# Attention logits from float32r operands, with the decay rows in two parts, and head-pair copies moved one place up in the order

## The reference, cut to what matters

```
log_f = log_sigmoid(f_logit)                       # (tokens, heads)
cum   = cumsum(log_f over tokens)                  # per head
s     = q_t . k_s / sqrt(64) + (cum[t] - cum[s])   # logits, blocks of 128 query tokens
s     = where(s_pos <= t_pos, s, -inf)             # causal
p     = softmax(s);  out = p @ v
y_b   = out @ attn_w_out
merged = sigmoid(g_a) * y_a + sigmoid(g_b) * y_b ; merged @ w_out
```

## Time and profile before

| | us |
|---|---|
| median of 3 runs | 2123.0 (2119.06 to 2129.02) |
| the profiled execution's own time | 2125.95 |
| its span, first to last instruction | 2124.2 |
| TensorE busy in the span | 1950.9 (92%) |
| VectorE busy | 1540.6 (73%) |
| ScalarE busy | 984.4 (46%) |

### The profile page before, as it was taken

How to read it: one execution, slowest core, us unless ns; L and a number is a source line. 1 busy time by engine, 2 the same in 40 slices (tenths; PEclk the granted TensorE clock), 3 DMA queues, 4 the chain that set the end, 5 groups by cost and what they waited for, 6 DMA issues and landing times.

```text
span 2124.2 us, 34037 instructions
## 1 busy us (share of the span) xinstructions
PE 1950.9 (92%) x14000; PEld 1813.8 (85%) x14000; DVE 1540.6 (73%) x2265; ACT 984.4 (46%) x1551; POOL 245.0 (12%) x190
## 2 busy tenths in 40 slices
PE   6897999987979998998889998999899989998998
PEld 6796899987958997988879888998898889888997
DVE  5866688878556897688667666898777667666555
ACT  5523444454235444545443455444546543445444
POOL 1020011110201111111100000111111100001111
PEclk9998999989989999999989999999999989999999
DMA  5320599523215984445523345896444523244552
GB/s 206 119 98 21 195 341 359 215 100 114 85 54 225 357 328 166 169 161 236 234 103 120 120 156 208 339 374 252 145 172 170 183 96 140 100 169 147 181 179 100
DMA packets 53291, 384.23 MB, mean 181 GB/s; under 512 B 5904, under 2 KB 6032, under 8 KB 6928
## 3 DMA queue, kind: packets, MB, share of 16 engines
q1 hardware_dynamic: 53136, 382.05, 48.1%
HBM read 380.98 MB, written 1.05 MB: 180 GB/s over the span
## 4 chain that ended last, share of the span: by engine, by line
PE 72%; DVE 16%; ACT 6%; issue 4%; DMA 1%; SPq 0%; DVEq 0%; ACTq 0%
PE stream L436 14%; PE stream L437 14%; PE stream L438 14%; PE works L450 5%; PE works L451 5%; PE works L452 5%; DVE w_lo L1030 3%; ACT w_hi L775 3%; DVE mx L1139 2%; DMA raw<-w 1%; PE stream L488 1%; DVE mx L1227 1%; PE works L612 1%; PE stream L489 1%; PE works L697 1%
## 5 line engine op out<-in xcount | busy, mean ns | idle before, releaser
L436 PE MATMUL stream<-h_hi,w_hi 128*128 128x256 f32 x2976 | 854.5, 287 | 23.5 <-DVE w_lo L1030 23.3
L437 PE MATMUL stream<-h_lo,w_hi 128*128 128x256 f32 x2976 | 847.9, 285 | 0.0
L438 PE MATMUL stream<-h_hi,w_lo 128*128 128x256 f32 x2976 | 847.6, 285 | 0.0
L1030 DVE TENSOR_TENSOR w_lo<-raw,w_hi 128x1024 fp32r<-128x1024 f32 x572 | 736.2, 1308 | 145.8 <-ACT w_hi L775 119.4
L775 ACT ACTIVATE w_hi<-raw 128x1024 fp32r<-128x1024 f32 x572 | 588.3, 1050 | 131.7 <-PE works L452 82.0
L436 PEld LDWEIGHTS stream<-h_hi,w_hi 128*128 128x128 f32 x2976 | 576.9, 194 | 32.8 <-issue 29.9
L437 PEld LDWEIGHTS stream<-h_lo,w_hi 128*128 128x128 f32 x2976 | 577.3, 194 | 2.6 <-issue 0.5
L438 PEld LDWEIGHTS stream<-h_hi,w_lo 128*128 128x128 f32 x2976 | 576.9, 194 | 0.0
L1506 POOL TENSOR_TENSOR g_lo<-hid,g_hi 128x256 fp32r<-128x256 f32 x140 | 191.9, 1372 | 1589.9 <-ACT g_hi L805 1589.9
L933 ACT ACTIVATE gate_t<-stream 128x256 f32<-128x256 f32 x132 | 50.6, 384 | 408.0 <-PE stream L438 405.2
L450 PE MATMUL works<-w_hi,g_hi 128*128 128x512 f32 x528 | 207.5, 393 | 4.2 <-DVE w_lo L1030 4.1
(11 more groups left out here) (368 smaller groups left out, 2271.1 us busy)
## 6 DMA issues: line engine op xcount, KB each, us to landing
raw<-w SPq DMA_DIRECT2D x294, 1024.0 KB, 4.8
mx<-w SPq DMA_DIRECT2D x64, 1024.0 KB, 7.0
par<-p_in SPq DMA_DIRECT2D x2, 1110.0 KB, 7.5
x<-x_in SPq DMA_DIRECT2D x1, 1024.0 KB, 6.7
mx<-bt_in SPq DMA_DIRECT2D x2, 512.0 KB, 5.6
out<-x SPq DMA_DIRECT2D x4, 256.0 KB, 2.4
con<-const_in SPq DMA_DIRECT2D x1, 968.0 KB, 4.7
par<-p_in SPq DMA_DIRECT2D x1, 225.0 KB, 6.8
```

Source lines behind the costliest of these rows:

```text
L436: mm(o, hi, r_hi[:, kt, :], start=first, stop=False, skip_group_check=True)
L437: mm(o, hi, r_lo[:, kt, :], start=False, stop=False, skip_group_check=True)
L438: last = mm(o, lo, r_hi[:, kt, :], start=False, stop=end, skip_group_check=True)
L1030: v.tensor_tensor(w_lo[:, q % SLOTS, :], raw[:, chunk_of_unit[q] % RAWS, (q % 2) * UNIT:(q % 2 + 1) * UNIT], w_hi[:, q % SLOTS, :].bitcast ...
```

## The change

Three things change in the mixers of both second-kind layers, and one in the constant table.

1. The identity and one 128x128 penalty block are rounded to float32r tiles (`ident_r`, `pen_r`) by two ScalarE copies at the start of the program. The decay rows get a tile of their own, `cum_r`, with a high and a low part of 384 columns each, zeroed by one VectorE memset. At `cum`, ScalarE writes the high part as before; VectorE then waits for it and writes the low part (two instructions on 8 partitions).
2. `score` has five products instead of four: high part, low part (384 columns each) and penalty (256 columns, the one block read twice) as float32r products; the two products of q and k stay as they are. TensorE also waits for the low part and the two rounded tables.
3. `hout` 1 moves in front of `pair` 15, `hout` 2 in front of `glu` 1.
4. The constant table loses two blocks of the penalty and half of the row of times: 1552 columns instead of 1936, in the first transfer of the program.

```diff
-    ("pair", 15), ("norm_p", 6), ("score", 7), ("hout", 1), ("attend", 4), ("turnp", 5),
-    ("glu", 0), ("norm_p", 7), ("attend", 5), ("turnp", 6),
-    ("glu", 1), ("hout", 2), ("attend", 6), ("turnp", 7), ("hsplit", 0),
+    ("hout", 1), ("pair", 15), ("norm_p", 6), ("score", 7), ("attend", 4), ("turnp", 5),
+    ("glu", 0), ("norm_p", 7), ("attend", 5), ("turnp", 6), ("hout", 2),
+    ("glu", 1), ("attend", 6), ("turnp", 7), ("hsplit", 0),
...
-PC, NC = columns([("ident", P), ("triu", P), ("ones", P), ("m", 7 * P), ("pen", 3 * P), ("time", T), ("c", 8),
+PC, NC = columns([("ident", P), ("triu", P), ("ones", P), ("m", 7 * P), ("pen", P), ("time", T // 2), ("c", 8),
...
+        ident_r = sb("ident_r", [P, P], F32R)
+        pen_r = sb("pen_r", [P, P], F32R)
+        cum_r = sb("cum_r", [P, 2, 384], F32R)
...
-        cumrows = p2_(0, "c_im")[:, 0:384]
+        cum_hi, cum_lo = cum_r[:, 0, :], cum_r[:, 1, :]
...
                     pe.wait_ge(s_cm_done, 2 * (L + 1))
+                    pe.wait_ge(s_cl_done, 2 * (L + 1))
+                    pe.wait_ge(s_masks_done, 2)
...
-                    mm(o[:, 0:384], ident[:, i:i + 1].to_broadcast([P, P]), cumrows, start=True, stop=False,
-                       skip_group_check=True)
-                    mm(o[:, P:384], ident, c_("pen", P), start=False, stop=False, skip_group_check=True)
+                    pick = ident_r[:, i:i + 1].to_broadcast([P, P])
+                    mm(o[:, 0:384], pick, cum_hi, start=True, stop=False, skip_group_check=True)
+                    mm(o[:, 0:384], pick, cum_lo, start=False, stop=False, skip_group_check=True)
+                    mm(o[:, P:384].rearrange("p (a n) -> p a n", a=2), ident_r[:], pen_r[:].unsqueeze(1).to_broadcast([P, 2, P]),
+                       start=False, stop=False, skip_group_check=True)
...
+            f(ident_r[:], ident, ACT.Copy).then_inc(s_masks_done, 1)
+            f(pen_r[:], c_("pen"), ACT.Copy).then_inc(s_masks_done, 1)
...
-                        f(cumrows[0:8, a:a + n_], works[0:8, 2, 0:n_], ACT.Copy, scale=-1.0).then_inc(s_cm_done, 1)
+                        f(cum_hi[0:8, a:a + n_], works[0:8, 2, 0:n_], ACT.Copy, scale=-1.0)\
+                            .then_inc(s_cm_done, 1)
...
-                    v.memset(cumrows, 0.0).then_inc(s_cum_zero, 1)
+                    v.memset(cum_r[:].bitcast(F32), 0.0).then_inc(s_cum_zero, 1)
...
+                elif kind == "cum":
+                    dve.wait_ge(s_cm_done, 2 * (L + 1))
+                    dve.wait_ge(s_cum_zero, L + 1)
+                    for a, n_ in ((0, T), (T, P)):
+                        v.scalar_tensor_tensor(cum_lo[0:8, a:a + n_], works[0:8, 2, 0:n_], -1.0,
+                                               cum_hi[0:8, a:a + n_].bitcast(F32), ALU.mult, ALU.subtract).then_inc(s_cl_done, 1)
```

More of the change, by code:

```diff
@@ L328, in build @@
          s_pe_f, s_f_dve, s_f_act, s_lf_done, s_pe_ck, s_cm_done, s_pe_vt, s_vt_sb, s_pe_sc,
-         s_bu_half, s_cum_zero, s_y_out, s_nm_done, s_p_exp, s_p_norm, s_pe_pt, s_pt_sb, s_pe_at, s_pads, s_dt_done) = (
+         s_masks_done, s_cl_done, s_bu_half, s_cum_zero, s_y_out, s_nm_done, s_p_exp, s_p_norm, s_pe_pt, s_pt_sb, s_pe_at, s_pads, s_dt_done) = (
             sem(n) for n in """pe_stat sq_done hf_done hhi_done hlo_done gate_th hid_done ghi_done glo_done
@@ L337, in build @@
             tab_sin pe_bu z_sum z_in wv_done s_sum pe_y g_in g_tanh
-            pe_f f_dve f_act lf_done pe_ck cm_done pe_vt vt_sb pe_sc bu_half cum_zero y_out nm_done p_exp p_norm
+            pe_f f_dve f_act lf_done pe_ck cm_done pe_vt vt_sb pe_sc masks_done cl_done bu_half cum_zero y_out nm_done p_exp p_norm
             pe_pt pt_sb pe_at pads dt_done""".split())
@@ L1617 @@
         "ident": np.eye(P), "triu": (idx[:, None] <= idx[None, :]), "ones": np.ones((P, P)),
-        "m": np.concatenate(masks, axis=1), "pen": -np.concatenate([np.zeros((P, P)), future, future], axis=1),
-        "time": np.broadcast_to(np.arange(T)[None, :], (P, T)), "c": tiles(a["c_2"][0]),
+        "m": np.concatenate(masks, axis=1), "pen": -future,
+        "time": np.broadcast_to(np.arange(BLK)[None, :], (P, BLK)), "c": tiles(a["c_2"][0]),
         "final": tiles(a["final_norm_g"])})
```

## The result

The changed kernel took 2112.95 us as a median of 7 runs (2109.08 to 2114.48). The kernel before, run beside it, took 2129.02 us (2119.06 to 2133.53, 7 runs). The ratio is 0.9921, with a 95% interval of 0.9904 to 0.9939: 16.8 us faster. The prediction was 2104.0 us with a range up to 2112: the measured time lies 1 us outside it. The saving had been forecast as 19.3 us.

The account below looks back on a forecast made before the run. TensorE was taken to bound the mixers; savings of 9.8 + 7.5 + 1.5 + 0.5 = 19.3 us from 2125.95 gave 2106.7, and 2.95 less as a median gave 2103.7, predicted as 2104 us, range 2097 to 2112.

Parts of the forecast that it names:

- The products of the logits: In each of 16 scores, three float32r products take 0.56 us instead of 1.17, saving 9.8 us in all.
- third: In the scores, exposed weight loads make the new products cost 1.12 us; 0.8 us saved, 2113 us; chance 0.04.
- fourth rival: In the scores, float32r on spread or repeated operands costs as much as float32, losing 10.2 us; 2125 us; chance 0.04.
- the second: Scores gain less than TensorE saves because VectorE is still busy; half of 9.8 us lost, 2109 us; chance 0.07.
- The copies moved up: At attend 4 and 6 in both mixers, the waits for the hout copy go, saving 7.5 us.
- the first rival: The wait moves on to attend 5 and 6 in both mixers, costing 4 us; 2108 us; chance 0.15.
- The clock: Behind the first mixer's wait at attend 4, the fall to half clock goes too: 1.5 us, bounds 0 and 3.
- The low part, the zeroing and the waits: At cum and the program's start, the added work and waits cost nothing, covered by idle time of the engines.
- The first transfer: At the program's start, the shorter constant table lets the first weights land 0.46 us earlier, counted as 0.5 us.
- The sum: Over the whole kernel, savings of 19.3 us against the profiled execution's 2125.95 us, giving 2106.7 us.
- the step from the sum to a time: For the whole kernel, 2106.7 us was lowered by 2.95 us to a median of 2103.7, predicted as 2104.

Follow-up runs that it names:

- the kernel with the logits alone: Changed kernel with the two hout copies back at their old places, float32r logits and shorter table kept; 2121.66 us, ratio 0.9963 to the kernel before.
- the reordered kernel: Changed kernel with cum placed behind fwd 2 instead of in front of it; 2108.74 us, ratio 0.9909 to the kernel before.
- the stacked one: Changed kernel with high and low decay parts on different rows of one product instead of two products; 2106.5 us as median of 12 runs.

## Why the prediction missed, point by point

**The products of the logits**: right. 0.57 us instead of the 0.56 worked out, with the 384 columns at 0.18 where the middle of two rows had given 0.17. That saves 0.60 us in each of 16 scores, 9.6 of 9.8 us. The operands that no row showed, a spread column and a block read twice, cost no more than the rows of plain ones gave, within 0.01 us, and the third and fourth rival are out. So is the second, since the scores' saving arrived whole: 4.2 us for seven scores in the first mixer of the kernel with the logits alone. The Trainium skill ("TensorE: Matmul & The Clock Gate", "What overlaps and what doesn't") has a weight load overlap the product in flight only where the two use different row groups; the trace disagrees: in the rows above three products on the same 128 rows start 0.18 us apart, and each load of 0.19 us for the next one starts with a product (1214.96 and 1215.14) and runs beside it.

**The copies moved up**: right. Both waits went in both mixers and none came in their place; 3.6 us measured in the clean second mixer against 3.74. The margins at `attend` 5 and 6 were 0.8 and 1.0 us instead of the 0.5 and 0.4 worked out, and the first rival is out.

**The clock**: right in part. The fall behind the wait at `attend` 4 in the first mixer shows in all three profiles of before and in that of the logits alone, and in none of the eight profiles of kernels with the copies moved. But the wait alone doesn't bring it: it stands in the second mixer too, where no fall follows, and in the kernel with the shorter table, where `attend` 4 waits 1.71 us in the first mixer and the clock stays full. The kernel before, and that one, in the 3 us behind the wait:

```profile
1219.00:1222.00 3.00, 3.00 (x12) 2.28 (x13) 0.00 (x0) 0.72 (x4) 0.00 (x0) 0.50 0.71 300
```
```profile
1219.00:1222.00 3.00, 3.00 (x27) 3.00 (x26) 0.29 (x1) 2.24 (x6) 0.00 (x0) 1.00 0.54 227
```

So the 1.5 us were those of one profiled execution. And the term took this one place alone, while the clock falls in others. In three of the four profiles of the changed kernel, a new low stretch lies in the second mixer behind `score` 0, with TensorE busy throughout:

```profile
1779.00:1783.00 4.00, 4.00 (x22) 4.00 (x23) 1.82 (x7) 2.25 (x4) 0.00 (x0) 0.57 0.39 164
```

It costs 1.5 us (180.9 against 179.4 without it) and gives back what was gained. Over all profiles, it stands in five of the eight second mixers with float32r logits and in none of the five without, but in the first mixers only once in thirteen, in the kernel before. Whether the quicker logits favour it, or whether this is chance, stays open.

**The low part, the zeroing and the waits**: right, at no cost, as the reordered kernel showed. VectorE's two instructions took 0.54 us up to the next start (1147.99 to 1148.53), estimated at 0.65. But the cover was nearly used up: 0.23 us were left.

**The first transfer**: mis-sized. The first rounding began at 11.05 us, 0.20 earlier than in the earlier trace rows, not 0.46; over all profiles it was 10.96 to 11.05 in the changed kernel against 11.23 to 11.29 before. The step turned all bytes taken away into time of the landing. Why only half of it arrived is not shown. And a gain of 0.2 us can't be seen in a front that scatters by 4.

**The sum** was 19.3 us. The mixers of the first two profiles gave 17.1 us (377.3 against 360.2), of which 9.6 are the logits; the rest, 7.5, is about 7.2 of the copies (twice 3.6), 1.5 that the clock gave at `attend` 4 and 1.5 that it took behind `score` 0. The start gave 0.2. The comparisons of the runs gave 16.8, 19.6 and 17.7 us (from 0.9921, 0.9908 and 0.9917). Their mean is 18.0, so the saving was right in size.

**What failed is the step from the sum to a time.** It said: "The median of the three runs lies 2.95 us below that execution, which puts the changed kernel at 2103.7 as a median." The sum made against the profiled execution, 2106.7 us, was within 4 us of the 20 runs' 2110.3. The median of three runs of 2119, 2123 and 2129 us was taken for the centre; the centre is 2129. Two of the three were low draws, of a kind that 12 of 50 runs are, and they shifted the whole forecast by 6 us. The range had no term for that: it took the distance of the three runs from their median, and not how far such a median may lie from the centre. With 2129 for the base, the same steps end at 2109.7 us, 0.6 below the median of the 20 runs. The rest of the miss is scatter: the 7 runs of the result, at 2112.95, lay 2.7 us above that median, which itself lies inside the range, with the same wrong base.

## What to carry to other kernels

Where TensorE sets the end, a plain float32 product is dear (here 0.64 us for 384 columns against 0.18 in float32r), and splitting its moving operand into two float32r parts pays even with the second product; better still, put both parts on different rows of one product, if the useful rows are few. A copy that frees a buffer belongs at the place where its input is ready, not just in front of its user: behind `score` 7 it also swallowed the 0.6 us that this score had gained. Before a saving is set against a median, look how far the single runs lie apart: with three runs 10 us apart and an effect of 19, the base is the largest unknown, and a ratio says more than a time.

## What was not expected of the hardware

- The same program over the same 25 us, with TensorE busy 24.81 us both times, started 196 or 221 products, at a mean granted clock of 0.80 or 0.93. That alone moved a mixer by 3 us, and the first layer came out at 410.8, 412.8 or 414.8 us with no change in it.
- The granted clock was at 0.57 in a stretch of 4 us in which TensorE was busy for 4.00 us. Ahead of it TensorE had been busy for 13.90 of 14 us at full clock, last with the products of `bu` 3 on 32 rows, so a long idle time ahead is not needed for a fall. A wait of 1.7 us was not enough for one either: the same wait was followed by a clock of 0.50 or of 1.00.
- VectorE writes float32r rows on partitions 32 to 39 from rows 0 to 7 as it writes rows 0 to 7: the two instructions took 0.61 us in the changed kernel and 0.61 us in the stacked one.
